# Early unnormalised row stores, a diagonal in place of scaling, gathers ahead of the branch, and Silu as the experts' gate

## The reference, cut to what matters

```python
x2 = rms_norm(h, norm2)                       # h: residual stream after out-projection
g_logits = x2 @ w_rg + b_rg                   # 4 groups, top 1
e_logits = (x2 @ w_re + b_re).reshape(-1, 4, 4)   # 4 experts in each group, top 2 of the chosen group
top_w = softmax(top_v) * g_w                  # weights of the two experts
for e in range(16):
    hid = silu(x2 @ w_g[e]) * (x2 @ w_u[e])   # 1024 -> 512
    out = out + gates[:, e:e + 1] * (hid @ w_d[e])
```

## Time and profile before

| what | value |
|---|---|
| median of 3 runs | 913.15 us (908.6 to 914.84) |
| profiled execution | 911.01 us, of it span 909.1 us |
| busy: PE, DVE, ACT, POOL | 838.4, 660.1, 475.4, 88.0 us |
| DMA | 178.29 MB, mean 196 GB/s |
| first expert product | at 613.64 us of the span |

### The profile page before, as it was taken

The page is one execution under the profiler, slowest core; times in us unless marked ns, Lnnn a source line. Parts: engine busy times, 40 slices in busy tenths (PEclk is TensorE's granted clock), DMA queues, the critical chain, the costliest instruction groups (busy, mean ns, idle before and its releaser), DMA issues.

```text
span 909.1 us, 19485 instructions
## 1 busy us (share of the span) xinstructions
PE 838.4 (92%) x8314; PEld 556.0 (61%) x8314; DVE 660.1 (73%) x934; ACT 475.4 (52%) x678; POOL 88.0 (10%) x90
## 2 busy tenths in 40 slices
PE   5999999999999998999999999939899989988882
PEld 4444784845856554444444469919788678777651
DVE  4759599799756787444435355566799999998987
ACT  5433673322666654232332335534778878788742
POOL 8000000002000000000000000010222313122000
PEclk9999999999999999999999999957999999999996
DMA  9732023434961115934234254465899999999972
GB/s 243 176 93 70 2 71 94 116 94 116 229 183 36 42 39 171 352 105 128 85 107 118 79 148 182 153 254 198 324 356 395 400 379 402 386 384 373 379 285 96
DMA packets 122641, 178.29 MB, mean 196 GB/s; under 512 B 13373, under 2 KB 98677, under 8 KB 114358
## 3 DMA queue, kind: packets, MB, share of 16 engines
q1 hardware_dynamic: 116272, 162.76, 52.5%
q0 software_dynamic: 6000, 13.67, 5.7%
q10 hardware_dynamic: 278, 0.56, 0.2%
HBM read 170.73 MB, written 14.39 MB: 204 GB/s over the span
## 4 chain that ended last, share of the span: by engine, by line
PE 62%; DVE 14%; DMA 13%; ACT 7%; issue 4%; POOLq 0%; ACTq 0%; POOL 0%; SPq 0%; DVEq 0%
PE bank L1044 19%; PE bank L1046 18%; PE bank L1045 18%; DVE arena L1887 5%; DMA arena<-in_moe_wu 3%; DMA arena<-in_moe_wd 3%; DMA arena<-x_rows,token_of 3%; ACT arena L914 2%; PE bank L1162 1%; PE bank L1275 1%; DVE arena L2002 1%; DMA arena<-y_rows 1%; DMA x_rows<-arena 1%; ACT arena L999 1%; DMA y_rows<-arena,row_of 1%
## 5 line engine op out<-in xcount | busy, mean ns | idle before, releaser
L1045 PE MATMUL bank<-arena 128*128 128x96 f16 (+4 forms) x2488 | 527.7, 258 | 0.0
L1044 PE MATMUL bank<-arena 128*128 128x128 f16 (+6 forms) x1976 | 456.7, 271 | 16.2 <-DVE arena L1887 6.5
L1046 PE MATMUL bank<-arena 128*128 128x128 f16 (+6 forms) x1976 | 455.5, 270 | 0.0
L1045 PEld LDWEIGHTS bank<-arena 128*128 128x128 f16 (+1 forms) x2488 | 248.7, 100 | 66.5 <-issue 0.7
L1044 PEld LDWEIGHTS bank<-arena 128*128 128x128 f16 (+2 forms) x1976 | 197.0, 100 | 110.4 <-issue 24.2
L1046 PEld LDWEIGHTS bank<-arena 128*128 128x128 f16 (+2 forms) x1976 | 196.4, 100 | 77.3 <-issue 0.7
L1887 DVE SCALAR_TENSOR_TENSOR arena<-arena 128x2048 f16<-128x2048 f32 x94 | 213.1, 2287 | 33.0 <-ACT arena L914 32.9
L914 ACT ACTIVATE arena<-arena 128x2048 f16<-128x2048 f32 x94 | 176.0, 1907 | 15.1 <-DMA arena<-in_moe_wu 7.6
L663 ACT ACTIVATE arena<-arena 128x1024 f16<-128x1024 f32 (+1 forms) x91 | 91.4, 1008 | 101.8 <-PE bank L1046 68.5
L1581 DVE SCALAR_TENSOR_TENSOR arena<-arena 128x1024 f16<-128x1024 f32 (+1 forms) x91 | 104.2, 1162 | 12.2 <-ACT arena L663 10.9
L1044 PE MATMUL bank<-beat,arena 128*128 128x96 f16 x512 | 72.1, 213 | 4.1 <-DVE arena L1887 4.0
(11 more groups left out here) (293 smaller groups left out, 770.8 us busy)
## 6 DMA issues: line engine op xcount, KB each, us to landing
arena<-in_moe_wg SPq DMA_DIRECT2D x32, 1024.0 KB, 18.0
arena<-in_moe_wu SPq DMA_DIRECT2D x32, 1024.0 KB, 19.6
arena<-in_moe_wd SPq DMA_DIRECT2D x32, 1024.0 KB, 20.0
arena<-in_w_gate SPq DMA_DIRECT2D x32, 512.0 KB, 3.8
arena<-in_w_in SPq DMA_DIRECT2D x31, 512.0 KB, 3.8
arena<-in_w_branch SPq DMA_DIRECT2D x32, 192.0 KB, 3.4
y_rows<-in_c_tab SPq DMA_DIRECT2D x4, 1024.0 KB, 11.3
arena<-in_w_out SPq DMA_DIRECT2D x8, 512.0 KB, 3.9
```

Source lines behind the costliest of these rows:

```text
L1044: pe.matmul(outb, lhs[0], rhs[0], start=first, stop=False, skip_group_check=True)
L1045: pe.matmul(outb, lhs[0], rhs[1], start=False, stop=False, skip_group_check=True)
L1046: return pe.matmul(outb, lhs[1], rhs[0], start=False, stop=last_, skip_group_check=True)
```

## The change

The rows `hg` are stored as they are made, slice by slice, without 1/rms. Lines 941 and 942 go. 1/rms of each token is carried beside its number: for experts 0 and 1 it comes out of the same near product, for the others it is stored to HBM (`rstd_rows`) and gathered by a second indirect DMA. POOL (for experts 0 and 1 VectorE) builds a diagonal from it, and x_transposes becomes a product with that diagonal. Token numbers are kept minus NOWHERE, so that an empty slot comes out as NOWHERE without a second column. The near one-hots are made one per expert straight from the rank bank. The gathers of experts 0 and 1 stand ahead of the branch, in two buffers. Root's table is loaded early. The split of chunk 5 moves ahead of the branch, the wide one-hots and the weights into it; in each step of ScalarE and VectorE the split comes first. The gate is ACT.Silu. The core of the diff, behind the tables in the order SP, POOL, ScalarE, TensorE, VectorE:

```diff
-WARM = 12
+WARM = 6
+PRE = 1
-NOWHERE = 65536
+NOWHERE = 2 * T
...
-    half[:, 0:P] = r[:, None] < r[None, :]
+    half[:, 0:P] = (r[:, None] < r[None, :]) - float(NOWHERE) * np.eye(P)
...
-        onehot = view(9216, NT, P * NE // 2).bitcast(F16)
+        onehot = view(9216, NT, CAP * NE // 2).bitcast(F16).rearrange("p t (c e) -> p t c e", e=NE)
+        onehot_near = [view(XS + 768 + NT * CAP * e, NT, CAP) for e in range(NEAR)]
+        xg = [arena[:, 8192:8192 + D], arena[:, 12288:12288 + D]]
...
         def x_at(c):
-            if e + 1 < NE and hf and kind == ("u" if e < NEAR else "g"):
+            if c == 0:
+                return 1
+            if c == STEPS.index(("d", 0, 0)):
+                return 2
+            if NEAR <= e < NE - 1 and hf and kind == "g":
                 return e + 1
...
-            for c in range(READY, READY + FIRST):
-                sp_.wait_ge(S("split_done"), splits_ahead(c))
+            for m in range(KD):
+                sp_.wait_ge(S("hg_ready"), m + 1)
+                sp_.dma_start(x2_rows[:, m * P:(m + 1) * P].rearrange("(t p) n -> p t n", p=P), hg[:, :, m * P:(m + 1) * P]
+                              ).then_inc(S("x2_stored"), 16)
+                for i in SPLIT_AT.get(m - 1, ()):
+                    sp_.wait_ge(S("split_done"), splits_ahead(READY + i))
+                    stage_load(READY + i)
+            sp_.wait_ge(S("out_full"), KD)
+            for c in (READY - 2, READY - 1):
                 stage_load(c)
...
-            for t in range(NT):
-                sp_.wait_ge(S("x2_ready"), t + 1)
-                sp_.dma_start(x2_rows[t * P:(t + 1) * P, :], xs[:, t, :]).then_inc(S("x2_stored"), 16)
+            sp_.wait_ge(S("rstd2_ready"), 1)
+            sp_.dma_start(rstd_rows((1, P), (P, NT), (1, 1)), rstd2.unsqueeze(2),
+                           allow_slow_non_contiguous=True).then_inc(S("rstd_stored"), 16)
+            sp_.wait_ge(S("token_read"), NEAR)
+            stage_load(READY + FIRST)
...
+            pool.wait_ge(S("x2_stored"), 16 * KD)
+            pool.wait_ge(S("token_read"), 1)
+            gather_rows(0)
+            pool.memset(xg[1], 0.0).then_inc(S("pool_step"), 1)
...
+            gather_rows(1)
             pool.wait_ge(S("path_known"), 1)
...
+                        gather_rows(e)
+                        pool.indirect_dma_start(out=rslot[0:CAP, e:e + 1], out_offset=None, in_=rstd_rows((1, T), (1, 1)),
                                                 in_offset=bass.IndirectOffsetOnAxis(ap=token_of[0:CAP, e:e + 1], axis=0),
...
+                        pool.wait_ge(S("xg_landed"), rows_landed(e))
+                        pool.tensor_scalar(slot_diag[e % 2][0:CAP, :], ident[0:CAP, 0:CAP], rslot[0:CAP, e:e + 1], None, ALU.mult
+                                           ).then_inc(S("slot_diag"), 1)
...
+                if m == KD - 2:
+                    link(act.activation(stat[:, 2, 0:1], ones[:, 0:1], ACT.Sqrt))
...
-            act.wait_ge(S("rstd2_ready"), 1)
-            for t in range(NT):
-                act.activation(xs[:, t, :], hg[:, t, :], ACT.Copy, scale=stat[:, 3, t:t + 1]).then_inc(S("x2_ready"), 1)
+            for i in range(FIRST, FIRST + PRE):
+                split(i)
...
+                    if FIRST + PRE <= c + LOOK < CUT:
+                        split(c + LOOK)
                     if kind == "g" and hf:
...
-                        act.activation(sgr, ps[2 * (e % 2)][:, 0:KH * CAP], ACT.Tanh, scale=0.5 / WSCALE).then_inc(S("sg_ready"), 1)
+                        act.activation(sgr, ps[2 * (e % 2)][:, 0:KH * CAP], ACT.Silu, scale=1.0 / WSCALE).then_inc(S("sg_ready"), 1)
...
-                            last = pe.transpose(ps[6 + j][:, k * CAP:(k + 1) * CAP], xg[0:CAP, 4 * P * j + k:4 * P * (j + 1):4],
-                                                ident[0:CAP, 0:CAP])
+                            last = pe.matmul(ps[6 + j][:, k * CAP:(k + 1) * CAP], x_gathered(e)[0:CAP, 4 * P * j + k:4 * P * (j + 1):4],
+                                             slot_diag[e % 2][0:CAP, :], start=True, stop=True)
...
-                    if kind == "g" and not hf:
-                        pe.wait_ge(S("xlo_done"), 2 * (e + 1))
+                    if kind == "g":
+                        pe.wait_ge(S("xlo_done"), 2 * e + hf + 1)
...
-            link(tt(tied, other, own, ALU.is_ge))
-            link(tt(ahead, other, own, ALU.is_gt))
-            link(tt(tied, tied, lower.rearrange("p (i j) -> p i j", j=EPG).unsqueeze(1).to_broadcast(wide), ALU.mult))
-            link(tt(ahead, ahead, tied, ALU.max))
+            link(tt(lead, other, own, ALU.subtract))
+            link(tt(ahead, lead, beaten_by.rearrange("p (i j) -> p i j", j=EPG).unsqueeze(1).to_broadcast(wide), ALU.is_ge))
...
-            link(stt(flat(rank[:, :, :]), ps[5][:, 0:NT * NE], 1.0, flat(sel16[:, :, :]), ALU.add, ALU.mult))
-            link(ts(rank[:, :, :], rank[:, :, :], -1.0, None, ALU.add))
-            sig("onehot_ready", tt(onehot_near, slots.rearrange("p (c e) -> p c e", e=NE)[:, :, 0:NEAR].unsqueeze(1)
-                                   .to_broadcast([P, NT, P, NEAR]),
-                                   rank[:, :, 0:NEAR].unsqueeze(2).to_broadcast([P, NT, P, NEAR]), ALU.is_equal))
+            for e in range(NEAR):
+                dve.wait_ge(S("token_full"), e + 1)
+                sig("token_read", ts(token_of[0:CAP, e:e + 1], near_token(e)[:, 0:1], float(NOWHERE), None, ALU.add))
+                link(dve.tensor_copy(rslot[0:CAP, e:e + 1], near_token(e)[:, 1:2]))
+                if e + 1 < NEAR:
+                    sig("onehot_ready", tt(*near_views(e + 1), ALU.is_equal))
+                tell("slot_diag", ts(slot_diag[e][0:CAP, :], ident[0:CAP, 0:CAP], rslot[0:CAP, e:e + 1], None, ALU.mult))
+            for i in range(FIRST, FIRST + PRE):
+                split(i)
...
+                    if c == 0:
+                        for t in range(NT):
+                            tell("onehot_ready", tt(*onehot_views(t), ALU.is_equal))
+                        x_lo(1)
-                    if c == 4:
+                    if c == 3:
                         all_slots()
+                    if FIRST + PRE <= c + LOOK < CUT:
+                        split(c + LOOK)
+                    if c == 1:
+                        tell_lists()
...
-                        link(stt(sgr, sgr, 1.0, ps[b0][:, 0:KH * CAP], ALU.add, ALU.mult))
-                        tell("h_ready", stt(hid, sgr, 0.5 * HSCALE / WSCALE ** 2, ps[b0 + 1][:, 0:KH * CAP],
+                        if e:
+                            dve.wait_ge(S("hlo_done"), e)
+                        tell("h_ready", stt(hid, sgr, HSCALE / WSCALE, ps[b0 + 1][:, 0:KH * CAP],
                                             ALU.mult, ALU.mult))
```

More of the change, by code:

```diff
@@ L176, in constants @@
     sq[:, 3 * P:3 * P + 4] = r[:, None] + P * np.arange(NT)[None, :]
-    sq[:, 3 * P + 4:3 * P + 20] = np.tril(np.ones((EPG, EPG)), -1).reshape(-1)
+    sq[:, 3 * P + 4:3 * P + 20] = np.where(np.tril(np.ones((EPG, EPG)), -1), 0.0, np.finfo(np.float32).tiny).reshape(-1)
+    sq[:, 3 * P + 20:3 * P + 40] = np.repeat([0.5, 1.5], [EPG, NE])
     for h in range(IDX_HEADS):
@@ L317, in build @@
         gain2 = arena[:, 48268:48268 + D]
-        onehot = view(9216, NT, P * NE // 2).bitcast(F16)
-        onehot_near = view(39436, NT, P * NEAR // 2).bitcast(F16).rearrange("p t (c e) -> p t c e", e=NEAR)
-        slots = view(19456, P * NE // 2).bitcast(F16)
-        xg = arena[:, 8192:8192 + D]
+        onehot = view(9216, NT, CAP * NE // 2).bitcast(F16).rearrange("p t (c e) -> p t c e", e=NE)
+        onehot_near = [view(XS + 768 + NT * CAP * e, NT, CAP) for e in range(NEAR)]
+        hg_dense = view(XS, NT, D)
+        slots = view(19456, P * NE // 2).bitcast(F16).rearrange("p (c e) -> p c e", e=NE)
+        xg = [arena[:, 8192:8192 + D], arena[:, 12288:12288 + D]]
+        slot_diag = [view(39820 + CAP * i, CAP) for i in range(2)]
         def token_half(v):
@@ L406, in build, with near_token, rows_landed, rstd_rows @@
         scratch, x2_rows, y_rows = d["bias_scratch"], d["x2_rows"], d["y_rows"]
+        def near_token(e):
+            return ps[7][0:CAP, 2 * e:2 * e + 2]
+        def rows_landed(e):
+            return 16 * (1 + 2 * max(e + 1 - NEAR, 0))
+        def rstd_rows(*shape):
+            return bass.AP(scratch.tensor, 0, list(shape))
         def y_bank(e):
@@ L538, in _ @@
             with sp_.Else():
-                for i in range(READY):
+                for i in range(READY + 1):
                     sp_.wait_ge(S(f"stage_landed{i}"), 32 if i < FIRST else 16)
-                sp_.wait_ge(S("split_done"), FIRST)
-                sp_.wait_ge(S("token_full"), 1)
+                sp_.wait_ge(S("split_done"), FIRST + PRE)
+                sp_.wait_ge(S("xg_landed"), 16)
+                sp_.wait_ge(S("xg1_landed"), 16)
+                sp_.wait_ge(S("x2_stored"), 16 * KD)
```

(21 more changed lines are left out.)

181 lines of the change are left out of this document (91 added, 90 removed).

## The result

The changed kernel took 942.78 us (median of four runs, 940.88 to 943.81), the kernel before 912.42 us beside it: ratio 1.034, 95% interval 1.032 to 1.036. It is 3.4% slower where 903 us was forecast, and it lies far outside the range of 896 to 909. Its profiled execution has a span of 941.2 us, 32.1 us more than the 909.1 us of before.

What follows compares the result with a forecast made beforehand. DMA work was taken to set the end, with VectorE nearly full. Gains 9.5 + 1.1 - 0.5 = 10.1 us took the profiled 911.0 to 900.9; plus 2.1 to the median gave 903.0 us, range 896 to 909.

Steps and rivals of the forecast that it cites:

- the transposes as products with a diagonal: Experts' transposes on TensorE: fp32 products cost 0 extra, bounded by 0 and 0.6 us, the last overlapping with evictions.
- 64 list products, 4.1 us: TensorE's list products ahead of the third gather: 4.1 us, ending at 622.6, third gather near 625.
- First gather: POOL's first gather of expert rows: starts at 596.6 and lands 4.6 us later, at 601.2, for 610.9 previously.
- the 14 gathers: Added indirect DMAs of 1/rms, 96 x 4 bytes each: 0.5 us cost taken, between 0 and 14 us.
- The near products: Token products on TensorE for the first experts, small fp32 instead of fp16: 0.4 to 0.9 us.
- The DMA bound: Among the experts VectorE is nearly full, but total DMA work sets the end, with periods growing to 18.22 us.
- The 9.5 us to be won at the start: Start of the experts: 20.1 us earlier DMA idle plus 8.1 us work moved ahead, less 18.7 us idle remaining.
- the port between POOL and VectorE: Rival, chance 0.05: POOL's diagonal holds VectorE up to one split, 2.29 us, costing 1 to 4 us: 906.
- The late refill: Rival, chance 0.22: one-hots, lists and weights inside the branch delay splits; 3 to 5 us more DMA idle: 907.
- POOL's latency, the rival on the slow side: Rival, chance 0.06: rows, 1/rms and diagonal take over 16 us, making transposes late; at 18 us, 927.
- the sign that the prediction names: Among the signs that would show the forecast wrong: TensorE waiting for slot_diag.
- the table load ahead of the router: Sqrt's table loaded on ScalarE at m = 6; router's first VectorE step at 590.8, semaphore 590.9, instead of 591.57.

Runs made afterwards that it cites:

- products in before: Kernel before the change, with only the experts' transposes made as ordinary fp32 products with the identity: 924.94 us, ratio 1.0165.
- lists of 128 columns: Changed kernel, with 48 of the 64 list products loading 128 columns of the one-hot instead of 96: 935.48 us.
- no store of 1/rms: Changed kernel without SP's store of 1/rms to HBM and POOL's wait for it, so the output is another: 932.39 us.
- plain transposes: Changed kernel, with true transposes against the identity instead of products with the diagonal; diagonals still built, rows unscaled: 914.89 us.
- three undone: Changed kernel with true transposes (rows unscaled), 48 of 64 list products loading 128 columns, and no 1/rms store to HBM: 904.17 us.
- also without POOL: Changed kernel with true transposes, 128-column list loads, no 1/rms store, and no POOL gather of 1/rms, wait or diagonal product: 902.22 us.
- plain, without POOL: Changed kernel with true transposes, rows unscaled, and without POOL's gather of 1/rms, its wait and its diagonal product: 912.12 us.
- mixed: Changed kernel, whole computation kept: 1/rms comes with list products, ScalarE scales rows in place (later for experts 1 and 3), true transposes, 128-column list loads: 903.65 us.
- the first experiment: Changed kernel, with true transposes against the identity instead of products with the diagonal; rows unscaled, POOL still builds diagonals: 914.89 us.

## Why the prediction was wrong

Third step and steady part of all the kernels, side by side:

| kernel | third step at | third to 15th | a chunk's landing, issued 760 to 800 (median) | what sets the steady part |
|---|---|---|---|---|
| before | 665.4 | 204.3 | 27.1 | periods 16.03, then DMA, 18.2 and 18.3 |
| after | 681.3 | 219.5 | 8.0 | TensorE, 17.11, POOL once |
| products in before | 672.5 | 211.1 | 14.0 | TensorE, 17.11 |
| lists of 128 columns | 675.2 | 218.4 | 9.1 | TensorE, POOL once |
| no store of 1/rms | 674.3 | 218.2 | 9.3 | TensorE, POOL once |
| plain transposes | 669.9 | 202.1 | 22.8 | periods 15.45, POOL twice |
| three undone | 660.0 | 203.0 | 27.6 | 15.45, POOL once, then DMA to 18.2 |
| also without POOL | 658.5 | 203.5 | 27.8 | 15.45, then DMA to 18.6 |
| plain, without POOL | 663.8 | 206.4 | 27.8 | 15.45, then DMA to 18.4 |
| mixed | 660.1 | 203.1 | 23.1 | 16.48, TensorE and the scaling |

*The failed step: the transposes as products with a diagonal, "0 and 0.6 us bound it; I take 0".* One expert's set takes 4.05 us at the first expert instead of 1.57, and 3.93 instead of 1.17 once the experts run. The upper end came from one row, line 1099, itself a product with a diagonal, read as 275 ns a product. That row already showed the price: four tiles by eight blocks are 32 products there, and the row counts 64 records. Two times 275 ns a product, by eight, would have made 4.4 us a set. TensorE had 133.27 us of 140 busy, so some 0.8 us of room in a period of 16.03 us, against 2.8 us more a set. The prediction asked only whether the evictions cover the products, not what TensorE's own sum becomes. That it becomes the bound is shown twice, by taking the products out (27.9 us) and by putting them alone into before (17.11 us).

*64 list products, 4.1 us.* Mis-sized: 11.7. The duration was taken over from loads of 128 columns for loads of 96. Loading 128 in 48 of the 64 gave 6.2 us back at the third step.

*First gather, "lands 4.6 us later, at 601.2".* Its issue was near (598.2 for 596.6), the landing at 608.1. The 2 KB store of 1/rms isn't in the prediction at all: it prices the 14 gathers and passes over the store that feeds them. Without it the landing is 4.2 us, and 7.0 us come back at the third step. The first product stands at 612.01 in after, for 605.5 predicted and 613.64 before; without the store it stands at 605.95.

*The near products*, 0.4 to 0.9 us a set predicted, are eight records for four products and took 1.44 us each: the same mistake about fp32, and small, since the first gather was issued only 1.6 us late.

*The DMA bound* was right about before, and about three of the four kernels with plain transposes and no scaling in place: their periods grow from 15.45 to 18.2 us and more, with landings of 27 us, and their steady parts lie within 203.0 and 206.4 us. In the first experiment POOL's two stretches stand in its place. It was the wrong bound for the changed kernel, whose chunks land after 8 us where those of before take 27. The 9.5 us to be won at the start were found in part, 5.4 us with the three undone and 6.9 without POOL's scaling, counted at the third step. The mixed version's 903.65 us is next to the forecast of 903.0 by chance: it has another period, set by TensorE and ScalarE.

*Rivals.* One that came true in part is the port between POOL and VectorE, priced at one split, 2.29 us. The product was held over three, 6.66 and 7.51 us, and what waited was TensorE and not VectorE. The Trainium skill ("SBUF — State Buffer", Who interferes with whom) states the exclusion, and the traces agree: POOL's product ends 0.4 us behind the third split. The late refill came true by its sign and not by its cause: what held the third gather was the first gather and TensorE's list products, for which VectorE sat idle 9.57 us. POOL's latency, the rival on the slow side, came about only once: from the issue of a gather to the end of POOL's product it took 5.2 to 11.8 us for thirteen experts, and 17.0 us for the expert whose product was stretched to 7.51 us, where the sign that the prediction names, TensorE waiting for slot_diag, shows with 4.54 us. No rival had TensorE as the bound, and none joined a slow start to it.

*What held:* the table load ahead of the router (VectorE's first step at 591.7 for 590.9 predicted), the selection at 594.3 for 593.5, the four wide one-hots with 3.55 us, Silu's one load of 1.28 us without a drain, slice stores under cover (the first gather waited for its token numbers and not for them), and that line 2043 is worth nothing while another engine is the bound. The table load for Exp starts at 593.54, right behind ScalarE's split, takes 1.28 us, and the activation behind it starts at 594.83, so there is no sign of the drain that the Trainium skill ("ScalarE: Activation LUTs", What ACT_TABLE_LOAD costs) adds to it.

## What to carry to other kernels

Where one form of instruction takes another's place, count the records of the nearest row against the instructions that the code issues, and then add the new time to the busy sum of its own engine: an edit that hides behind evictions may still fill the engine that carries the rest. Compare kernels by a step that all have, once per expert: it parts a start that is late from a period that is long, and the two are paid for separately. A DMA share of 1.0 doesn't make DMA the bound: look at whether landings grow and whether an engine waits for them. Of a transfer look at its pieces and not at its size, and of a weight load at its form.

## What the runs showed of the hardware

- An ordinary fp32 product leaves two records where a transpose against the same operand shape leaves one: 2 x 397 ns for 283 ns (96x96), weight loads 330 ns for 218. A set of eight takes 3.93 us for 1.17.
- In the list products loading weights of 128x96 fp16 takes 278 ns, of 128x128 164 to 168 ns, and the products behind them 320 for 203 ns, at a granted clock of 0.63 and 0.75. In the experts' products of the mixed version, at a granted clock of 1.00, the loads take 0.12 and 0.10 us.
- A store of 512 separate elements of 4 bytes landed after 13.7 us; beside it the DMA engines are called busy for 0.59 and move 45 GB/s, and a gather of 96 rows takes 9.9 us for 4.2.
- A POOL product of 0.53 us (96x96) can last as long as a run of three of VectorE's splits beside it: 6.66 us and 7.51 us were seen.
- Two kernels with the same DMA share (1.01 from 660 to 800 us) had different bounds: in before a chunk landed after 27.1 us and ScalarE waited for landings, with the products put into it after 14.0 us and ScalarE did not.
